# A two-layer decoder step on one core: three edits around the sample attention and the output projection

## What is computed

```
def layer(x, l, ...):
    h = rms_norm(x, g_ffn1_pre[l])
    x = x + 0.5 * rms_norm(swiglu(h, w_ffn1_in[l], w_ffn1_out[l]), g_ffn1_post[l])
    mix, ... = mix_layer(rms_norm(x, g_mix_pre[l]), ...)     # w_in, four head groups, w_out
    x = x + rms_norm(mix, g_mix_post[l])
    ...                                                      # the second feed-forward block

# in mix_layer, after h @ w_in: mLSTM (A), gated linear attention (B),
# dilated window attention (C), stick-breaking attention (D)
    hc = window_fn(qc, kc, vc)        # sample rows: softmax over 2048 cached keys and 8 new ones, three dilations
    hd = sb_fn(qd, kd, vd, b_sb)      # sample rows: stick-breaking over 16 pages of 128 cached keys and 8 new ones
    mixed = jnp.concatenate([ha, hb, hc, hd], -1)
    return mixed @ w_out, ...

def stick_breaking_attention(q, kc, vc, q_pos, bias):
    z = einsum('bqhd,bkhd->bhqk', q, kc) * HEAD_DIM ** -0.5 + bias
    log_beta, log_keep = log_sigmoid(z), log_sigmoid(-z)     # masked
    later = cumsum(log_keep, reverse=True) - log_keep
    return einsum('bhqk,bkhd->bqhd', exp(log_beta + later), vc)
```

## Time and profile before

| what | us |
|---|---|
| median of three runs | 2505.3 |
| lowest and highest run | 2501.26, 2509.03 |
| the profiled execution | 2508.6 |
| span of the profiled execution | 2506.9 |
| PE busy in it | 2340.8 |
| DVE busy, ACT busy | 1192.0, 930.7 |

### The profile page before, as it was taken

How to read it: one execution, slowest core, us unless ns; L and a number is a source line. 1 busy time by engine, 2 the same in 40 slices (tenths; PEclk the granted TensorE clock), 3 DMA queues, 4 the chain that set the end, 5 groups by cost and what they waited for, 6 DMA issues and landing times. The chain is left out here.

```text
span 2506.9 us, 44904 instructions
## 1 busy us (share of the span) xinstructions
PE 2340.8 (93%) x17622; PEld 2084.8 (83%) x17622; DVE 1192.0 (48%) x2080; ACT 930.7 (37%) x1671; POOL 144.3 (6%) x195
## 2 busy tenths in 40 slices
PE   7999999989888799999899999999898887999997
PEld 7999998756556599999899999977565566999997
DVE  6343273254575565342463434622646565643425
ACT  6223242223325554222352323321333265542333
POOL 0000010011222000000000000100213210000000
PEclk8999999989998899999999999999898898999998
DMA  5233333145765543233333333420658545333233
GB/s 140 68 85 84 101 111 124 51 134 175 208 174 172 146 144 86 67 94 85 91 86 83 84 84 102 146 86 21 193 163 238 166 133 179 98 85 84 76 103 95
DMA packets 384957, 290.97 MB, mean 116 GB/s; under 512 B 51808, under 2 KB 368392, under 8 KB 384272
## 3 DMA queue, kind: packets, MB, share of 16 engines
q1 hardware_dynamic: 368128, 234.08, 33.4%
q0 software_dynamic: 16128, 54.54, 7.1%
q10 hardware_dynamic: 528, 0.02, 0.0%
HBM read 274.99 MB, written 13.58 MB: 115 GB/s over the span
## 5 line engine op out<-in xcount | busy, mean ns | idle before, releaser
L218 PE MATMUL ps<-h_hi,w_hi 128*128 128x288 f32 x2400 | 718.2, 299 | 24.1 <-PEq L174 16.8
L219 PE MATMUL ps<-h_lo,w_hi 128*128 128x288 f32 x2400 | 710.0, 296 | 0.0
L220 PE MATMUL ps<-h_hi,w_lo 128*128 128x288 f32 x2400 | 709.8, 296 | 0.0
L242 DVE TENSOR_TENSOR w_lo<-w_raw,w_hi 128x2048 fp32r<-128x2048 f32 x145 | 332.4, 2292 | 341.0 <-ACT w_hi L236 340.9
L218 PEld LDWEIGHTS ps<-h_hi,w_hi 128*128 128x128 f32 x2400 | 452.2, 188 | 30.4 <-issue 24.7
L219 PEld LDWEIGHTS ps<-h_lo,w_hi 128*128 128x128 f32 x2400 | 452.2, 188 | 1.0
L220 PEld LDWEIGHTS ps<-h_hi,w_lo 128*128 128x128 f32 x2400 | 452.0, 188 | 0.0
L236 ACT ACTIVATE w_hi<-w_raw 128x2048 fp32r<-128x2048 f32 x145 | 276.7, 1908 | 163.6 <-PE ps L220 159.3
L218 PE MATMUL ps<-f_a_hi,w_hi 128*128 128x288 f32 x1024 | 302.7, 296 | 0.0
L220 PE MATMUL ps<-f_a_hi,w_lo 128*128 128x288 f32 x1024 | 301.6, 295 | 0.0
L219 PE MATMUL ps<-f_a_lo,w_hi 128*128 128x288 f32 x1024 | 301.5, 294 | 0.0
(11 more groups left out here) (345 smaller groups left out, 3170.9 us busy)
## 6 DMA issues: line engine op xcount, KB each, us to landing
w_raw<-in_w_ffn_in SPq DMA_DIRECT2D x132, 512.0 KB, 5.2
w_raw<-in_w_ffn_out SPq DMA_DIRECT2D x80, 512.0 KB, 5.0
sa_vn<-in_cache_sb_v SPq DMA_DIRECT2D x256, 128.0 KB
w_raw<-in_w_in SPq DMA_DIRECT2D x52, 512.0 KB, 4.4
sa_vn<-in_cache_win_v SPq DMA_DIRECT2D x96, 128.0 KB
w_raw<-in_w_out SPq DMA_DIRECT2D x24, 512.0 KB, 6.7
sa_kn_early<-in_cache_win_k POOLq DMA_DIRECT2D x72, 128.0 KB
sa_vn<-in_cache_win_v SPq DMA_DIRECT2D x16, 512.0 KB
```

What stands on the lines that cost most here:

```text
L218: pe.matmul(out, stat_hi, mov_hi, start=start, stop=False, skip_group_check=True)
L219: pe.matmul(out, stat_hi, mov_lo, start=False, stop=False, skip_group_check=True)
L220: return pe.matmul(out, stat_lo, mov_hi, start=False, stop=stop, skip_group_check=True)
L242: dve.tensor_tensor(E["w_lo"][:, slot], E["w_raw"][:, slot], E["w_hi"][:, slot].bitcast(F32), ALU.subtract).then_inc(S["w_lo"], 1)
```

## The change

There are three edits.

1. **Weights and gathers.** PE gets a function `tensor_behind`, too. Turning weights and gathering rows moves there, so that both come after the main step behind the tick; the values stay in the tick and come before them. The copies of the turned weights, ACT's and DVE's, and ACT's copy of the gathered rows move into `scalar_behind` and `vector_behind`, ahead of what these held.
2. **Semaphores.** The semaphores of a stage get fixed numbers from 103 on, those of the mixers and of the sample attention one run of numbers. `clear` is unchanged; the number of its barriers follows from the numbers.
3. **First chunk of the output projection.** The first weight chunk is split in two halves of 128x1024. ACT and DVE make the first half, then four blocks of the activations, then the second half and the other four blocks. PE waits for the first half before its first matmul (`part_lo`), and for the second (`w_lo`) at the fifth block of columns.

```diff
@@ stage
-        S = dict(**{s: st.enter_context(nc.semaphore(f"{name}_{s}")) for s in sems.split()})
+        S = {s: st.enter_context(nc.semaphore(f"{name}_{s}", first + n)) for n, s in enumerate(sems.split())}
...
@@ post_tensor
-        pe.wait_ge(S["w_lo"], n + 1 - warm)
+        if n > 0:
+            pe.wait_ge(S["w_lo"], n + 1 - warm)
...
@@ tensor_tick
-        for m in G["turn_at"].get(t, ()):
-            turn_weights(pe, chunks[m])
-        if t - 1 in G["ends"]:
-            gather_rows(pe, G["ends"][t - 1])
         for m, n in G["value_at"].get(t, ()):
             value_unit(pe, m, n)
+
+    def tensor_behind(pe, t):
+        for m in G["turn_at"].get(t, ()):
+            turn_weights(pe, chunks[m])
+        if t - 1 in G["ends"]:
+            gather_rows(pe, G["ends"][t - 1])
...
     def scalar_tick(act, t):
         if t < U:
             copy_keys_a(act, t)
+
+    def scalar_behind(act, t):
         for m in G["turn_at"].get(t, ()):
             if m % 2 == 0:
                 copy_weights_a(act, chunks[m])
...
-
-    def scalar_behind(act, t):
         for q in rows_at(t, 1):
...
+    def vector_behind(dve, t):
         for m in G["turn_at"].get(t, ()):
             if m % 2 == 1:
                 copy_weights_b(dve, chunks[m])
-
-    def vector_behind(dve, t):
...
@@ mixers
-            weave(pe, "tensor")
+            weave(pe, "tensor", side["tensor_behind"])
...
@@ output
+                if q == 0 and k == 0:
+                    pe.wait_ge(S["part_lo"], 1)
+                if q == 0 and k == KC // 2:
+                    pe.wait_ge(S["w_lo"], 1)
...
+            act.activation(split_part(E["w_hi"], 0), split_part(E["w_raw"], 0), ACT.Copy).then_inc(S["part_hi"], 1)
             for half in range(2):
-                split_hi(act, S, E, half)
+                if half == 1:
+                    split_hi(act, S, E, half)
                 for c in range(KC):
+                    if half == 0 and c == KC // 2:
+                        act.activation(split_part(E["w_hi"], 1), split_part(E["w_raw"], 1), ACT.Copy).then_inc(S["w_hi"], 1)
...
+            dve.wait_ge(S["part_hi"], 1)
+            dve.tensor_tensor(split_part(E["w_lo"], 0), split_part(E["w_raw"], 0), split_part(E["w_hi"], 0).bitcast(F32),
+                              ALU.subtract).then_inc(S["part_lo"], 1)
...
```

More of the change, by code:

```diff
@@ L145, in constants, with stage @@
     return c
+PAGE_SEM, FIRST_SEM = 99, 103
 @contextmanager
-def stage(nc, name, sems):
+def stage(nc, name, sems, first=FIRST_SEM):
     with ExitStack() as st:
-        S = dict(**{s: st.enter_context(nc.semaphore(f"{name}_{s}")) for s in sems.split()})
+        S = {s: st.enter_context(nc.semaphore(f"{name}_{s}", first + n)) for n, s in enumerate(sems.split())}
         st2 = ExitStack()
@@ L539, in early_upto, with split_part @@
     return min(len(J.early), 2 * (q - first))
+def split_part(x, part):
+    return x[:, 0, part * (SLOT // 2):(part + 1) * (SLOT // 2)]
 def post_tensor(pe, E, S, St, a_hi, a_lo, nk, base, warm, operand):
@@ L881, in _, with project @@
             post_vector(dve, E, S, St, F, FF, FF, 1, "ffn", Jt)
-def project(nc, E, M, l, w_in, kind, side, early):
+def project(nc, E, M, l, w_in, kind, side, early, first_sem):
     sems = (WEIGHT_SEMS + " ".join(f"open_{n}" for n in FIN_SEMS.split())
@@ L889, in project @@
     BANKS = 6
-    with stage(nc, "pr", sems) as (S, sb, block):
+    with stage(nc, "pr", sems, first_sem) as (S, sb, block):
         So = opening(S)
@@ L2349, in side_plan, with sample_attention @@
                 events=events, scored=scored, valued=valued)
-def sample_attention(nc, st, E, M, l, I, C):
+def sample_attention(nc, st, sem, E, M, l, I, C):
     ps = E["ps"]
@@ L2376, in sample_attention @@
             "out_units rows_ready ones_ready")
-    S = {s: st.enter_context(nc.semaphore(f"sa_{s}")) for s in sems.split()}
+    S = {s: sem(f"sa_{s}") for s in sems.split()}
     def sb(n, shape, dt=F32):
@@ L2608, in tensor_tick @@
                 score_new(pe, chunks[q["chunk0"] + q["chunks"] - 1])
+        for m, n in G["value_at"].get(t, ()):
+            value_unit(pe, m, n)
+    def tensor_behind(pe, t):
         for m in G["turn_at"].get(t, ()):
@@ L2612, in tensor_tick @@
             gather_rows(pe, G["ends"][t - 1])
-        for m, n in G["value_at"].get(t, ()):
-            value_unit(pe, m, n)
     def copy_keys_a(act, n):
@@ L2773, in sample_attention @@
                 keys=[landed(False, U - SLOTS + x) for x in range(SLOTS)], sync=sync_tick, gpsimd=gpsimd_tick, tensor=tensor_tick, scalar=scalar_tick, vector=vector_tick,
-                scalar_behind=scalar_behind, vector_behind=vector_behind)
+                tensor_behind=tensor_behind, scalar_behind=scalar_behind, vector_behind=vector_behind)
 TICK_RATE = dict(ml=0.565, ro=0.3, gl=0.43, pa=0.222)
@@ L2842, in output @@
 def output(nc, E, M, l, I, g_next, load_next):
-    with stage(nc, "ou", STAGE_SEMS + "mix_hi mix_lo x_loaded pages_moved") as (S, sb, block):
+    with stage(nc, "ou", STAGE_SEMS + "mix_hi mix_lo x_loaded pages_moved part_hi part_lo") as (S, sb, block):
         St = ending(S)
@@ L2876, in _ @@
         def _(dve):
+            dve.wait_ge(S["part_hi"], 1)
+            dve.tensor_tensor(split_part(E["w_lo"], 0), split_part(E["w_raw"], 0), split_part(E["w_hi"], 0).bitcast(F32),
+                              ALU.subtract).then_inc(S["part_lo"], 1)
             for half in range(2):
-                split_lo(dve, S, E, half, half + 1)
+                if half == 1:
+                    split_lo(dve, S, E, half, half + 1)
                 for c in range(KC):
+                    if half == 0 and c == KC // 2:
+                        dve.wait_ge(S["w_hi"], 1)
+                        dve.tensor_tensor(split_part(E["w_lo"], 1), split_part(E["w_raw"], 1),
+                                          split_part(E["w_hi"], 1).bitcast(F32), ALU.subtract).then_inc(S["w_lo"], 1)
                     dve.wait_ge(S["mix_hi"], KC * half + c + 1)
@@ L2907, in mixing @@
         with ExitStack() as st:
+            taken = []
             def sem(n):
-                return st.enter_context(nc.semaphore(n))
+                taken.append(n)
+                return st.enter_context(nc.semaphore(n, FIRST_SEM + len(taken) - 1))
             M["ml_stored"], M["gl_stored"] = sem("ml_stored"), sem("gl_stored")
             M["mx"] = {n: sem(n) for n in ("ml_bias", "ml_keep", "ro_consts")}
-            side = sample_attention(nc, st, E, M, l, I, C)
+            side = sample_attention(nc, st, sem, E, M, l, I, C)
             early_left = place(nc, "mx_left", LEFT, [P, LEFT_WORDS])
@@ L2929, in early @@
                 sp.dma_start(M["sin"], C["sin"]).then_inc(M["mx"]["ro_consts"], 16)
-            project(nc, E, M, l, I["w_in"], "ffn", side, early)
+            project(nc, E, M, l, I["w_in"], "ffn", side, early, FIRST_SEM + len(taken))
             for tag, names in (("ml", ML_SEMS), ("ro", RO_SEMS), ("gl", GL_SEMS), ("pa", PA_SEMS)):
@@ L3156, in program @@
             E[n] = carve(E["A"], k * NT, [P, NT])
-        E["page_sems"] = {f"page{x}": ctx.enter_context(nc.semaphore(f"page{x}")) for x in range(SLOTS)}
+        E["page_sems"] = {f"page{x}": ctx.enter_context(nc.semaphore(f"page{x}", PAGE_SEM + x)) for x in range(SLOTS)}
         E["spill"] = nc.dram_tensor("spill", (P, KC * NT), F32, kind="Internal").ap()
```

## The result

| | before | changed |
|---|---|---|
| median of 14 runs each, us | 2504.5 | 2517.3 |
| profiled execution, us | 2508.6 | 2517.2 |
| its span, us | 2506.9 | 2515.6 |

The ratio is 1.0044, with a 95% interval of 1.0032 to 1.0056: the change makes the kernel about 11 us slower (8 to 14); the two medians alone differ by 12.8. The prediction stood on a median of 2505.3 and said 2512. By the ratio that median would become 2516.3 (2513.3 to 2519.3), which lies between the forecast A (2512) and rival B (2517 to 2518), nearer to B; the interval holds B's time and just leaves out A's. The span of the profiled executions grew by 8.7.

What follows compares the result with a forecast made beforehand. PE was taken to bound the kernel, busy 93% of the span. Moving weights and gathers loses 11.2 us, the other two edits gain 4.2: +7.0 on the median of 2505.3 gives 2512; 8-in-10 range 2493 to 2519.

Steps and rivals of the forecast that it cites:

- forecast A: Whole kernel: the shared bank costs more than the turned waits bring, 2512 us; chance 0.40.
- rival B: Keys after T3 and T49: PE runs slower after the new pauses, 5.2 us more, 2517 to 2518; chance 0.18.
- the losing ticks: Mixers, ticks where next keys wait for the moved copy of turned weights: 13.1 us lost a layer.
- T3: Mixers: copy of W0 queues behind main step ml3, keys start 4.2 us later; 3.6 us lost a layer.
- T6: Mixers: DVE's copy of W1 queues behind two main-step instructions, second half of keys waits; 2.8 us lost a layer.
- T18: Mixers: PE's 2.48 us wait before turning weights vanishes behind main step ml24; 2.5 us won a layer.
- T30: Mixers: copy of W8 queues behind two instructions, one waiting for DVE, delaying keys; 3.5 us lost a layer.
- T49: Mixers: copy of W12 waits for four prompt-attention instructions, delaying keys; 2.3 us lost a layer.
- T53 to the end: End of mixers: the 2.34 us wait at T54 goes, DVE's copy is waited for less; 2.8 us won a layer.
- Rival C: Mixers: later waits make up for late keys; 2499 us with half the losses gone, 2486 with all; chance 0.30.
- rival D: Output projection: third chunk's load sets the time, semaphore and first-chunk edits bring nothing; 2516.5 us, chance 0.12.
- the paying ticks: Mixers, ticks where PE's wait before turning weights shrinks or goes: 7.5 us won a layer.

Runs made afterwards that it cites:

- e3: Weights and gathers moved only at the ticks where the prediction saw a gain, against the kernel before: ratio 0.9928, 18 us faster.
- e4: Weights and gathers moved only at the ticks where the prediction saw a loss, against the kernel before: ratio 1.0136, 34 us slower.
- e12: Weights and gathers moved at T3 alone, against the kernel before: ratio 1.0033, 8 us slower.
- e5: Changed kernel with four of PE's pauses filled by needless matmuls: ratio 1.0002 to the kernel before.
- e1: Kernel before with only the semaphore and first-chunk edits, weights and gathers not moved: ratio 0.9968, 8 us faster.

## Why the prediction was right, and where it was off

**The direction and the mechanism were right.** The forecast was a slower kernel in which keys wait for copies that now queue behind main steps. The list of waits, e3, e4 and e12 show it. That the total came within 4 us is in part luck, since the terms were further off and their errors oppose each other: the losing ticks cost 34 us for 26, the paying ones brought 18 for 15, and edits 2 and 3 brought 8 for 4.2. Term by term, in the traces:

| tick | forecast, us a layer | shift of the next keys, layer 0, layer 1 |
|---|---|---|
| T3 | 3.6 lost | 4.9, 4.4, and 2.4, 0.8 in the two ticks behind it |
| T6 (to the keys of T8) | 2.8 lost | 3.2, 3.1 |
| T10 | 1.0 won | 1.4, 1.4 |
| T14 (to the keys of T16) and T23 | 0.9 lost | 0.6, 0.6 |
| T18 | 2.5 won | 2.5, 5.5 |
| T26 | 0.8 won | 0.9, 0.2 |
| T30 | 3.5 lost | 3.6, 4.3 |
| T34 | 0.4 won | 1.3, 2.7 |
| T32 | none | 1.9 lost, 3.5 won |
| T49 | 2.3 lost | 2.3, 2.3, and 2.8, 0.0 in the tick behind it |
| T53 to the end (from the keys of T51) | 2.8 won | 0.6 lost, 1.1 won |

Shown are the ticks with a term in the prediction and T32; a shift of the next keys holds the changes of pace too. The places and signs hold in every row but two. At T32, where edit 1 moves nothing, only the pace differs. Of the last row the prediction missed a part: the last gather now comes behind all other matmuls of PE, some 0.7 us that nothing hides (2.49 us from PE's last products with `pa_left` to the end, for 1.81).

**The step that was mis-sized is the clock.** The prediction priced the pauses by their length and kept what follows them in rival B, at 0.18, with 1.3 us for each of T3 and T49. e5 shows that this belonged to the forecast. The clock falls at T3, and PE runs at the lower level for much of the next 30 us, not for the one tick of keys that B counted: from T3 to T8 it loses 5.0 us so in layer 0 and 2.4 in layer 1. Two readings of the prediction bear on this. "Layer 1 repeats layer 0 within a few tenths" was wrong, since the mixers of the two layers differ by 7 us; and the 0.63 us behind the pause at T18 was of layer 0, where the same four matmuls take 1.09 us behind the same pause in layer 1:

```profile
1862.98 1.09 PE L2557 MATMUL ps<-ident,sa_zs 128*128 128x128 f32 x4 [2.47 <-ACT sa_kt L2621]
```

The Trainium skill's page "Perfetto Trace Analysis", section "Matmul Optimizations", has the rule: the engine scales power by its use, so matmuls should come back to back. With it the trace agrees (a granted clock of 0.65 for 0.82), and so does e5, which only keeps PE busy.

**Edit 2** was sized by a wrong count (above): 0.91 a layer for about 1.2. **Edit 3** was right in its halves: 1.04 and 1.22 us had been worked out, 1.06 and 1.23 were measured (ACT at 885.24, DVE at 886.32 in the changed kernel), and the second half stalls nothing. The new wait for the third chunk was 0.2 and 1.25 us, for 0.5 and 1.0.

**Rival C** falls by e12, and **rival D** by e1, which has just the edits that D held for worthless and is 8 us faster. The 7 us forecast came out as 11: the pauses of edit 1 were about right in size, and the pace after them was left out.

## What to carry to other kernels

Before work is moved behind other work to hide a wait, look at who takes the result next: here the copy that frees a shared buffer went into an in-order queue behind work that itself waits, and the wait came back elsewhere, longer. Such a move is decided place by place and not by a rule for all; with the paying ticks alone the same edit is worth 18 us, whole it costs 8. And price a new pause of PE by the pace behind it too: a kernel with needless matmuls in the pauses is a quick way to measure that part.

## What the runs showed of the hardware that was not expected

A pause of the same length may or may not be followed by the lower clock. Beside T18 above (2.48 us), it shows at the end of the output projection of the kernel before, where PE pauses 3.52 us in both layers:

```profile
935.03 0.58 PE L218 MATMUL ps<-h_hi,w_hi 128*128 128x288 f32 x1 [3.52 <-PEq L174]
```
```profile
2171.52 0.37 PE L218 MATMUL ps<-h_hi,w_hi 128*128 128x288 f32 x1 [3.52 <-PEq L174]
```

The first product takes 0.58 us in layer 0, where the granted clock is 0.50, and 0.37 in layer 1, where it is 1.00. Two layers with the same instructions differ by 7 us in their mixers, and by such differences a span of one execution can mislead by as much as the whole change is worth.
